# Two-block transformer step: transposes of the recurrence rows issued ahead of the tile decay, copied by two engines, and the late weight units spread out behind them

## The reference, cut to what matters

```
mod = silu(c) @ ada_w + ada_b          # 1024 -> 6 x 1024: shift, scale, gate of both halves
h = rms_norm(x) * (1 + sc1) + sh1
z = h @ w_in
y_fox  = fox_mixer(z[:, :FOX_COLS])    # softmax heads
y_rwkv = rwkv7_mixer(z[:, FOX_COLS:])
x = x + g1 * ([y_fox, y_rwkv] @ w_out) # g1, sh2, sc2, g2 are the late two thirds of mod
h = rms_norm(x) * (1 + sc2) + sh2 ; x = x + g2 * moe_ffn(h)

# the recurrence, per head, S is 64 x 64
Sa = S a_t ; S = S * w_t + Sa b_t^T + v_t k_t^T ; y_t = S r_t
```

## Time and profile before

| | us |
|---|---|
| median of three runs | 1384.34 (1383.09 to 1384.56) |
| the profiled execution | 1383.96 |
| its span | 1381.5 |
| PE busy | 1313.4 (95%) |
| PE weight loads | 834.0 (60%) |
| DVE busy | 622.7 (45%) |
| ACT busy | 351.2 (25%) |
| POOL busy | 44.1 (3%) |

### The profile page before, as it was taken

One profiled execution on the slowest core, in us unless ns is written; L12 is line 12 of the kernel. 1 busy time (PEld: TensorE's weight loads), 2 busy tenths in 40 slices (PEclk: granted clock), 3 DMA queues, 4 the chain that ended last, 5 costly groups with the idle time before them and its releaser, 6 DMA issues.

```text
span 1381.5 us, 19977 instructions
## 1 busy us (share of the span) xinstructions
PE 1313.4 (95%) x7904; PEld 834.0 (60%) x7904; DVE 622.7 (45%) x1174; ACT 351.2 (25%) x609; POOL 44.1 (3%) x50
## 2 busy tenths in 40 slices
PE   5999998999899999999999999899999998999997
PEld 2545546965544444544444444578778566999985
DVE  2135377567422222222222222565448743677753
ACT  0202320012122221222222121454321112344542
POOL 0014200000000000000000000300000000000000
PEclk9999999999999999999999999999889999999998
DMA  9684284049299999999999996654611131455551
GB/s 342 235 263 152 101 366 160 2 117 407 112 397 422 419 409 423 412 418 418 417 414 421 407 419 240 230 166 153 135 19 61 62 122 61 153 183 185 186 197 73
DMA packets 96072, 341.19 MB, mean 247 GB/s; under 512 B 9248, under 2 KB 42680, under 8 KB 67213
## 3 DMA queue, kind: packets, MB, share of 16 engines
q1 hardware_dynamic: 85728, 321.16, 60.6%
q10 hardware_dynamic: 8109, 12.33, 3.4%
q0 software_dynamic: 2176, 6.86, 1.5%
HBM read 333.22 MB, written 1.05 MB: 242 GB/s over the span
## 4 chain that ended last, share of the span: by engine, by line
PE 86%; DVE 7%; DMA 4%; issue 1%; ACT 1%; ACTq 0%; DVEq 0%
PE bank L1890 17%; PE bank L1364 12%; PE bank L1906 9%; PE bank L1379 6%; PE bank L1380 6%; PE bank L1381 6%; PE bank L1852 3%; PE bank L1870 2%; PE bank L1872 2%; PE bank L1853 2%; DMA small<-in_norm_g 2%; PE bank L1350 2%; PE bank L1391 2%; PE bank L2280 2%; DMA ring<-in_w_in 1%; PE bank L1978 1%
## 5 line engine op out<-in xcount | busy, mean ns | idle before, releaser
L1364 PE MATMUL bank<-ring,xT 128*128 128x512 f32 (+1 forms) x416 | 180.4, 590 | 6.2 <-DVE xT L2454 2.3
L1364 PEld LDWEIGHTS bank<-ring,xT 128*128 128x128 f32 x416 | 79.5, 194 | 94.6 <-issue 84.3
L1906 PE MATMUL bank<-dn,tmp 128*64 128x512 f32 x528 | 120.6, 598 | 0.0
L3008 DVE TENSOR_TENSOR xT<-bank,mod 128x512 fp32r<-128x512 f32 x66 | 45.7, 692 | 157.9 <-ACT mod L1114 150.6
L3001 DVE SCALAR_TENSOR_TENSOR tmp<-silu_c,rc,bank 128x256 f32<-128x256 f32 x33 | 22.6, 685 | 196.8 <-ACT silu_c L1101 191.4
L1379 PE MATMUL bank<-mod,w_high 128*128 128x256 f32 x304 | 85.1, 280 | 0.0
L1380 PE MATMUL bank<-xn,w_high 128*128 128x256 f32 x304 | 85.1, 280 | 0.0
L1381 PE MATMUL bank<-mod,ring 128*128 128x256 f32 x304 | 84.8, 279 | 0.0
L3495 DVE TENSOR_TENSOR ring<-ring,w_high 128x1024 fp32r<-128x1024 f32 x60 | 70.7, 1221 | 21.7 <-ACT w_high L1299 20.2
L1906 PEld LDWEIGHTS bank<-dn,tmp 128*64 128x64 f32 x528 | 35.0, 136 | 68.3 <-issue 68.3
L1114 ACT ACTIVATE mod<-bank 128x512 fp32r<-128x512 f32 x64 | 38.2, 597 | 133.8 <-PE bank L1906 133.8
(11 more groups left out here) (654 smaller groups left out, 2296.9 us busy)
## 6 DMA issues: line engine op xcount, KB each, us to landing
dn<-in_exp_w_down SPq DMA_DIRECT2D x66, 1024.0 KB, 10.6
ring<-in_exp_w_gate SPq DMA_DIRECT2D x34, 1024.0 KB, 9.9
ring<-in_exp_w_up SPq DMA_DIRECT2D x34, 1024.0 KB, 12.5
gu_odd<-in_exp_w_gate SPq DMA_DIRECT2D x32, 1024.0 KB, 10.3
gu_odd<-in_exp_w_up SPq DMA_DIRECT2D x32, 1024.0 KB, 12.3
ring<-in_w_ffn_in SPq DMA_DIRECT2D x22, 1024.0 KB, 5.1
ring<-in_w_in SPq DMA_DIRECT2D x7, 2048.0 KB, 11.3
ring<-in_w_in SPq DMA_DIRECT2D x14, 912.0 KB, 4.9
```

The costliest lines, as they stand in the source:

```text
L1364: mm = pe.matmul(bank[lin_bank(o)][:, 0:n], lhs(k, t), ring[:, j % RING, k * n:(k + 1) * n], start=(k == 0), stop=(k == kt - 1 and not bias))
L1906: mm = pe.matmul(bank[6 + h][CHUNKS[c], :], act_eT[:, 0, k, CHUNKS[c]], dn[:, 2 * parity + c, lo:lo + BANK], start=(k == 0), stop=(k == D_ ...
L3008: dve.tensor_tensor(y_low[:, c], bank[6 + h][:, :], y_high[:, c].bitcast(F32), ALU.subtract)\
```

## The change

TensorE's `tile_decay` and units 8 to 11 no longer stand ahead of `til_transposes(0)`. The transposes start right behind `attend(7)`. Inside them, between the second and third pair, stand `tile_decay` (tile 0 only) and one late unit, with a wait for the copies of the first two pairs. The units are spread one by one: 8 in the transposes of tile 0, 9 behind them, 10 in the transposes of tile 1, 11 behind `transposed_grams(0)`, 12 behind `first_matrices(1)`, 13 behind `transposed_grams(1)`, 14 behind `first_transposes(1)`, 15 between the two `masked_source` of level 1. The wait for the late sums stands behind the second `masked_source`. ScalarE copies pairs 0 and 1 of each tile, VectorE pairs 2 and 3; ScalarE does tile 0 before the exponential and tile 1 behind the sigmoid. VectorE's wait for `rw_exp` stands behind `til_copies(0)`, `late_sums(0)` behind `first_masked(1)`, and `late_sums(1)` inside level 1, ahead of its operation for t = 1. No arithmetic is added or removed.

```diff
@@ -1022,10 +1022,21 @@
                     if h == 6:
                         in_copy(J_G, 1)
                     decays(h - 6)
+
+            def til_copies(t):
+
+                for pair in (0, 1):
+                    n = TP_TIL + 4 * t + pair
+                    act.wait_ge(tp_mm, n + 1)
+                    act.activation(tilT_of(t, pair),
+                                   bank[4 + n % 2][:, :].rearrange("p (i c) -> p i c", i=4), ACT.Copy).then_inc(tp_evac, 1)
+
+            til_copies(0)
             act.wait_ge(sc_mm, SC_CUM[2] + 1)
             act.activation(ws[:, 2, 0:4], bank[6 + SC_CUM[2] % 2][:, 0:4], ACT.Exp).then_inc(rw_exp, 1)
             act.wait_ge(lin_evac, after(J_G, 1))
             act.activation(z_fox[:, :, 1536:2048], z_fox[:, :, 1536:2048], ACT.Sigmoid).then_inc(fox_sig, 1)
+            til_copies(1)
             act.wait_ge(u_mm, 1)
             act.activation(rhs_u[:, 0, :], bank[0][:, :], ACT.Copy).then_inc(u_evac, 1)
             heads8 = lambda b: b.rearrange("p (h c) -> p h c", c=BS)
@@ -1558,8 +1569,6 @@
             attend(6)
             decay_sums(1)
             attend(7)
-            tile_decay()
-            late_units(2)
 
             halves = [slice(r * BS, (r + 1) * BS) for r in range(2)]
             block_of = lambda h: slice(h * BS, (h + 1) * BS)
@@ -1569,6 +1578,11 @@
 
                 pe.wait_ge(til_ready, t + 1)
                 for pair in range(4):
+                    if pair == 2:
+                        if t == 0:
+                            tile_decay()
+                        late_units(1)
+                        pe.wait_ge(tp_evac, TP_TIL + 4 * t + 2)
                     transposes([(i * P, (i + 1) * P, P, til(i, t)[:, pair * P:(pair + 1) * P]) for i in range(4)])
 
             def first_matrices(t):
@@ -1673,26 +1687,30 @@
                                    skip_group_check=True)
                 mm.then_inc(u_mm, 1)
 
-            late_units(2)
             til_transposes(0)
             late_units(1)
             pe.wait_ge(tp_evac, TP_TIL + 4)
             first_matrices(0)
             til_transposes(1)
             transposed_grams(0)
+            late_units(1)
             pe.wait_ge(fox_out, 1)
             first_transposes(0)
-            late_units(2)
             pe.wait_ge(tp_evac, TP_TIL + 8)
             first_matrices(1)
+            late_units(1)
             transposed_grams(1)
+            late_units(1)
             first_transposes(1)
             late_units(1)
             pe.wait_ge(sc_evac, SC_GRAM + 4 * T)
-            pe.wait_ge(late_summed, 2)
             for level in range(1, LAST + 1):
                 for t in range(T):
                     masked_source(t, level)
+                    if level == 1 and t == 0:
+                        late_units(1)
+                if level == 1:
+                    pe.wait_ge(late_summed, 2)
                 for t in range(T):
                     if level < LAST:
                         value_grams(T * (level - 1) + t)
@@ -2640,8 +2658,6 @@
             shifted_decay(1)
             decayed(1)
             dve.wait_ge(lerp_done, 4)
-            dve.wait_ge(rw_exp, 5)
-            dve.sem_inc(sc_evac, 1)
 
             def head_outputs():
 
@@ -2684,7 +2700,8 @@
 
             def til_copies(t):
 
-                for pair in range(4):
+                for pair in (2, 3):
+                    tp_n[0] = TP_TIL + 4 * t + pair
                     tp_copy(tilT_of(t, pair), P, BANK)
 
             def first_masked(t):
@@ -2742,17 +2759,20 @@
                 dve.tensor_tensor(late_rows[b], late_rows[b], bank[b][:, :], ALU.add).then_inc(late_summed, 1)
 
             til_copies(0)
+            dve.wait_ge(rw_exp, 5)
+            dve.sem_inc(sc_evac, 1)
             head_outputs()
             dve.wait_ge(late_used, late_order.index(EXTRA_SLOTS[1], 6) + 1)
             first_masked(0)
             til_copies(1)
             transposed_masked(0)
+            first_masked(1)
             late_sums(0)
-            first_masked(1)
             transposed_masked(1)
-            late_sums(1)
             for level in range(1, LAST + 1):
                 for t in range(T):
+                    if level == 1 and t == 1:
+                        late_sums(1)
                     dve.wait_ge(wkv_mm, wkv_count(t, level))
                     dve.tensor_tensor(amat[t], by_block(bank[6 + t][:, :]), folded(1 + level), ALU.mult)\
                         .then_inc(wkv_w, 1)
```

## The result

The changed kernel takes 1374.85 us (median of 4 runs, 1373.39 to 1377.38) against 1384.45 for the kernel before. The ratio is 0.9935, 95% interval 0.9917 to 0.9952: 9.0 us faster (6.6 to 11.5). A second set gave 1375.37 against 1384.90, ratio 0.9931 (0.9915 to 0.9946). The forecast, 1378.3 us, had the sign and the main mechanism; it was 3.5 us too high and its range ended 1 us above the result.

A forecast was written before the change was run, and what follows sets the result against it. PE was taken as held by slab landings, then DVE in series. 21.1 + 0.5 gaps + 1.65 clock gave 23.3 against 29.6 us; 6.0 saved from 1383.96 gave 1378.0, with the median's 0.4 offset 1378.3; range 1375.9 to 1381.2.

The forecast's parts named there:

- The new schedule's sum: From the end of attend(7) to level 1: the same PE operations add up to 21.1 us.
- ACT's copies: Tile 0, pairs 0 and 1: out by 196.2, 1.9 us before unit 8 ends, so PE's new wait is covered.
- its table load and sigmoid: ACT behind the moved exponential: they end at 199.7; the sigmoid serves only head gates behind the levels, cost zero.
- the late sum: Level 1: PE's wait covered by 0.1 us, the 1.02 us issue gone; 0.1 taken from 0 to 1.0 lost.
- loads 14 and 15: Late-unit slabs, slots released later: loss taken as 0 from bounds 0 and 0.7 us.
- the clock term: Stretch before level 1: one 3.3 us half-level piece stays and now loses 1.65 us.
- the clock stays up: Rival: no half-level piece in the stretch, 1.65 us more saved, 1376.7 us; chance 0.22.
- a second piece: Rival: another half-level piece in the stretch, or an equal loss, 1.65 us less saved, 1380.0 us; chance 0.20.
- Before, this cost nothing: Kernel before's stretch: the half-level piece was free because the next slab landed later anyway.
- the stall: Level 2: an unexplained 0.83 us PE stall could grow or double with earlier w_out loads; 0 to 0.8, taken as 0.
- the gaps: PE's remaining idle time in the new stretch: 0.5 us.
- the middle between 6.3 and 5.7: Two estimates of the stretch's saving, from summed operations (6.3 us) and from PE's busy time (5.7); 6.0 taken.

The follow-up runs named there:

- b1: Changed kernel with unit 15 and the second late sum ahead of level 1 again, TensorE waiting for the sum before the first masked source; 1377.90 us.
- b2: Changed kernel with tile_decay right behind the heads again, ahead of all transposes; 1376.68 us.
- b4: Changed kernel with tile 1's value products behind its updates in levels 1 to 4 and the w_out loads issued at the last level; 1373.70 us.
- c1: Kernel before with tile_decay behind the transposes of tile 0 and VectorE's wait for its exponential behind the copies; 1388.60 us.
- a2: Kernel before with only the copies shared, ScalarE pairs 0 and 1, VectorE 2 and 3, TensorE's order as before; 1381.77 us.
- a3: Changed kernel with all copies left to VectorE, so TensorE's new order alone; 1377.39 us.
- a4: Kernel before with the w_out loads issued at the last level instead of right behind the last late unit; 1381.46 us.

## Why the prediction was wrong

*Right.* The bound: PE's list was held by slab landings and then by DVE in series. The new schedule's sum, 21.1 us of PE work, met 21.42 busy. ACT's copies were covered (done at 194.5, unit 8 at 196.4), its table load and sigmoid harmless, the late sum covered, loads 14 and 15 in time. Nothing gained was given back behind: from level 4's first value product to the end the three traces of before take 1130.8 to 1131.4 us, those of the changed kernel 1130.5 to 1132.7.

*Wrong, the clock term.* "I keep one such piece" added 1.65 us; no trace of the changed kernel has one in the stretch. The size was right where it occurs (1.3 to 1.7 in b1, b2 and b4), and so was the picture of the rival "the clock stays up": 21.6 us of stretch against 22.2 measured, though its 1376.7 is 1.8 too high as well. The reason given, the one-column matmuls of `tile_decay`, does not hold as a rule: the clock stayed at 1.00 behind them in three traces, and fell in c1 without them. Which of the two cases comes varies between executions of the same order, as b1 and b4 show, and the forecast took one of them for certain.

The Trainium skill (TensorE: Matmul & The Clock Gate, Part 4: PE-mode transpose), by which transposes don't count for the gate as matmuls do, would have made a second piece likelier. Three traces with sixteen transposes in the first 4.7 us show none; it isn't refuted, as the kernels b1 and b4 with the same order there had one.

*Wrong, the kernel before's stretch.* "Before, this cost nothing" holds for the piece ahead of the slab landing only. I took 29.64 us from one trace; three give a mean of 30.0, as a piece behind the landing costs 1.25.

*Wrong in sign, the stall.* "It could grow or double: 0 to 0.8, I take 0" left out that it could shrink, and overlooked the one in level 1, which the trace at hand showed as 0.04 us only. On three traces each, level 1 gave 0.64 and level 2 0.53 us.

*Too small, the gaps and the work.* 0.5 of gaps foretold, 0.8 measured: two DVE handovers of 0.4. The work was 0.3 larger too, and these two took back a part of the clock term.

The account, three traces each: stretch 30.0 - 22.2 = 7.8, level 1 0.6, level 2 0.5: 9.0 us, against medians 9.5 to 9.6 apart. The spans of these traces are 9.7 us apart: another 0.9 lies ahead of the stretch, where the lists are the same and the half-level pieces were four against two, and 0.2 is lost behind. That 0.9 is luck of the executions traced; whether the medians hold the same isn't shown. Why a2, a3 and a4 measured 1.8, 1.2 and 1.4 us more than their traces give, against the means of the three of before, is open too.

Against the forecast of 6.0 it is 1.8 more in the stretch, 1.2 of stalls and some 0.6 of that rest. The 1.8 are 1.65 of clock and 0.4 of the base trace, less 0.6 of gaps and work, plus 0.4 because the forecast took the middle between 6.3 and 5.7. The range failed because its lower end was the best case of the stretch alone: by the stretch's 7.8 us the time would be some 1376.5, still inside, and the 1.2 us of stalls, taken as 0, carry it below.

## What to carry to other kernels

Where the chain charges a long time to a load, look for work in the same list that is ready and doesn't need it: the new order was worth 4.6 us (some 0.6 of it the late sum), and the second engine only then 2.9. A wait that is put into a list for another engine's copy should have a piece of independent work ahead of it (0.74 us of wait without, none with). Before a forecast, take a term that varies between executions (the clock, a stall without a releaser) with both signs, and ask whether it lies ahead of or behind the landing that sets the path.

## What the runs showed of the hardware

- The granted clock falls in one execution and not in the next of the same or nearly the same list: none in the stretch in three traces of the changed kernel, one piece of 3.4 us in b1 and b4. It fell in c1 with `attend(7)`, one unit and slab waits ahead and no one-column matmul of the decay. Single runs of one kernel span 4 to 11 us (before: 1380.8 to 1389.8, mean clock 0.982 to 0.987).
- A half-level piece of 3.4 us in the stretch cost 1.25 to 1.67 us where PE's list set the path, and nothing ahead of a slab landing for which PE waited another 1.14 us.
- PE stalled for 0.2 to 1.15 us without any releaser, in the midst of equal matmuls, during a 4 MB load (DMA share 1.03 in the pause) and again after its end (0.02), and not once in those levels when the load was issued later.
- A table load on ACT stood between copies and sigmoid as before (1.28 us); copies on either side of it needed no further one.
